# One ranking round in the router, router products spread over a wo2 unit, and waits moved in the experts' passes

## The reference, cut to what matters

```python
lg = t @ w_rg + b_rg                                  # 4 group scores per token
g_sel = argmax(lg);  w_grp = softmax(lg)[g_sel]
le = (t @ w_re + b_re).reshape(-1, 4, 4)              # 4 groups x 4 experts
le_g = le[g_sel]                                      # the chosen group's four
top_v, top_i = top_k(le_g, 2)
w_top = softmax(top_v) * w_grp                        # the two gates
for e in range(16):                                   # D = 1024, hidden = 512
    y = (silu(t @ w1[e]) * (t @ w3[e])) @ w2[e]
    acc += gate[e][:, None] * y
x = rmsnorm(x + g2 * acc, final_g)
```

## Time and profile before

| | |
|---|---|
| timed runs, median of 3 | 1209.31 us (1208.77 to 1213.37) |
| profiled execution | 1205.35 us |
| its span, first to last instruction | 1203.2 us |
| mean granted TensorE clock | 0.988 |
| TensorE busy | 1153.4 us (96%) |
| VectorE busy | 663.2 us (55%) |
| ScalarE busy | 499.2 us (41%) |
| GpSimd busy | 87.0 us (7%) |
| chain that ended last, by engine | PE 85%, DVE 9%, ACT 3%, issue 2% |

### The profile page before, as it was taken

The page is one execution under the profiler, slowest core; times in us unless marked ns, Lnnn a source line. Parts: engine busy times, 40 slices in busy tenths (PEclk is TensorE's granted clock), DMA queues, the critical chain, the costliest instruction groups (busy, mean ns, idle before and its releaser), DMA issues.

```text
span 1203.2 us, 21401 instructions
## 1 busy us (share of the span) xinstructions
PE 1153.4 (96%) x8936; PEld 996.9 (83%) x8936; DVE 663.2 (55%) x1143; ACT 499.2 (41%) x797; POOL 87.0 (7%) x92
## 2 busy tenths in 40 slices
PE   7999899999999989999999999999999899999996
PEld 6998789998979969999979889767899766665764
DVE  5777875588866476665555342775557531221223
ACT  5766523644374555544445222667344311111112
POOL 2451320000000100000100000000002000000000
PEclk9999999999999999999999999999999899999998
DMA  9544240443514746555564321302857899999980
GB/s 368 206 143 175 71 176 1 141 154 131 189 54 152 270 176 245 189 196 184 202 245 175 116 94 71 141 2 114 340 181 299 335 422 421 420 420 420 422 366 36
DMA packets 36204, 254.59 MB, mean 212 GB/s; under 512 B 4048, under 2 KB 4192, under 8 KB 5904
## 3 DMA queue, kind: packets, MB, share of 16 engines
q1 hardware_dynamic: 33552, 237.84, 51.4%
q0 software_dynamic: 2560, 15.42, 3.3%
HBM read 252.19 MB, written 1.05 MB: 210 GB/s over the span
## 4 chain that ended last, share of the span: by engine, by line
PE 85%; DVE 9%; ACT 3%; issue 2%; DMA 0%; DVEq 0%; ACTq 0%
PE bank L1374 13%; PE bank L712 12%; PE bank L706 12%; PE bank L707 12%; PE bank L668 5%; PE bank L1096 5%; PE bank L1182 4%; PE bank L1103 3%; PE bank L1386 2%; PE bank L759 2%; PE bank L1406 2%; PE bank L728 1%; PE bank L883 1%; DVE ring_low L2101 1%; PE bank L1284 1%
## 5 line engine op out<-in xcount | busy, mean ns | idle before, releaser
L2101 DVE TENSOR_TENSOR ring_low<-ring,w_high 128x2048 fp32r<-128x2048 f32 x104 | 238.0, 2290 | 160.8 <-ACT w_high L1629 160.7
L1629 ACT ACTIVATE w_high<-ring 128x2048 fp32r<-128x2048 f32 x104 | 199.1, 1915 | 281.5 <-PE bank L712 192.9
L706 PE MATMUL bank<-nT_high,w_high 128*128 128x256 f32 (+1 forms) x448 | 114.6, 295 | 0.0
L706 PEld LDWEIGHTS bank<-nT_high,w_high 128*128 128x128 f32 x448 | 84.2, 188 | 2.6 <-issue 2.4
L1374 PE MATMUL bank<-more,xs 128*64 128x256 f32 x768 | 84.6, 379 | 0.0
L1374 PEld LDWEIGHTS bank<-more,xs 128*64 128x64 f32 x768 | 58.7, 137 | 25.7 <-issue 2.2
L706 PE MATMUL bank<-hcl,w_high 128*128 128x256 f32 (+1 forms) x272 | 73.1, 306 | 0.0
L707 PE MATMUL bank<-hcl,w_high 128*128 128x256 f32 (+1 forms) x272 | 71.2, 299 | 0.0
L707 PE MATMUL bank<-nT_low,w_high 128*128 128x256 f32 (+1 forms) x272 | 64.7, 280 | 0.0
L706 PE MATMUL bank<-nMs,w_high 128*128 128x256 f32 x256 | 60.3, 280 | 1.4 <-DVE nMs L2493 1.4
L1096 PE MATMUL bank<-up,w_high 128*128 128x256 f32 x512 | 60.7, 276 | 0.0
(11 more groups left out here) (565 smaller groups left out, 2479.5 us busy)
## 6 DMA issues: line engine op xcount, KB each, us to landing
ring<-stream SPq DMA_DIRECT2D x163, 1024.0 KB, 4.9
more<-stream SPq DMA_DIRECT2D x60, 1024.0 KB, 18.7
more<-stream POOLq DMA_DIRECT2D x10, 1024.0 KB, 15.0
c<-constants_one SPq DMA_DIRECT2D x1, 1657.0 KB, 16.2
qc<-h_in SPq DMA_DIRECT2D x4, 272.0 KB, 3.8
c<-constants_two POOLq DMA_DIRECT2D x1, 1056.0 KB, 9.0
beside<-stream POOLq DMA_DIRECT2D x1, 1024.0 KB, 13.0
hT<-h_in POOLq DMA_DIRECT2D x1, 1024.0 KB, 6.0
```

The source lines that it names most:

```text
L706: nc.tensor.matmul(into[j], w, high_x(k), start=first, stop=False, skip_group_check=True)
L1629: A(w_high[:, d % 2, :], ring[:, s, :], ACT.Copy).then_inc(high_ready, 1)
L2101: TT(ring_low[:, s, :], ring[:, s, :], w_high[:, d % 2, :], sub).then_inc(low_ready, 1)
```

## The change

The diff does these things:

- Router: the two rankings become one over ten rows of four (two tokens' tiles of one group row and four expert rows), in a tile `beats` of its own that lies over `rB`, which is not in use then. The flag of the first group then selects both the experts' scores and their places. The arguments of the gates' exponentials become a function, `gate_arguments`, called after the first choices and the copy of the counts.
- wo2, unit 3: the products of blocks 0 to 5 are no longer made in one go halfway; block by block they are put among the products with the rounded weights (`among_wo2`). The sums of squares get a function of their own.
- Experts: the scatter waits for each half of the result by itself; in pass 0 the choices are turned before the hidden rows; the wait for the gates' column stands before the second half of the down products; in the extra pass only half of the scatter stands in front, the other half behind the up products; and the wait for the extra pass's gates moves from its start to where they are used.
- Pads: STAGGER grows from 16 to 48 words, a pad is added in front of `y_dsa_low`, and the pad under `more` grows by 16.

```diff
-STAGGER = 16
+STAGGER = 48
+        with ExitStack() as same:
+            beats = sb(same, "beats", 128, 10, 4, 8)
+                _stagger_dsa = sb(m, "stagger_dsa", 128, STAGGER)
...
                 for k in range(KT):
                     k_ready(k)
+                    among(k)
...
+            def router_squares(blocks):
+                dst = psum[banks.at["router"]]
+                pe.wait_ge(partial_ready, 3)
+                for k in blocks:
...
                 elif u == 3:
-                    router_blocks(range(6))
+                    router_squares([5])
+            def among_wo2(u, k):
+                blocks = {0: [0], 1: [1], 2: [2], 3: [3], 5: [4], 7: [5]}.get(k)
+                if u == 3 and blocks:
+                    router_blocks(blocks)
...
             router_blocks(range(6, KT))
+            router_squares(range(6, KT))
...
-            def scatter(count, signal=False, first=False):
-                pe.wait_ge(ys_ready, count * 2 + 2)
-                pe.wait_ge(spread_ready, count + 1)
-                for ft in range(KT):
+            def scatter(count, signal=False, first=False, fts=range(KT)):
+                if fts[0] == 0:
+                    pe.wait_ge(spread_ready, count + 1)
+                for ft in fts:
+                    if ft % 4 == 0:
+                        pe.wait_ge(ys_ready, count * 2 + 1 + ft // 4)
...
-                    scatter(count - 1)
+                    scatter(count - 1, fts=range(4))
...
+                if first:
+                    turn_choices()
+                    turn_hidden()
+                else:
+                    scatter(count - 1, first=(n == 1), fts=range(KT) if n < PAIRS else range(4, KT))
+                    turn_hidden()
+                    turn_choices()
...
-                pe.wait_ge(gate_slot_ready, count * 2 + 2)
                 for q in range(2):
+                    if q == 1:
+                        pe.wait_ge(gate_slot_ready, count * 2 + 2)
...
-                pe.wait_ge(gates_loaded, 2 * x + 2)
                 expert_pass(PAIRS, x, x + PAIRS, lambda qt: gate_of[:, qt, :])
...
+            five = rflat(0, 40).rearrange("p (s j) -> p s j", j=4)
+            step(TT(beats[:, :, :, 0:4], inner5, outer5, ALU.is_ge))
+            step(TT(beats[:, :, :, 4:8], inner5, outer5, ALU.is_gt))
+            step.settle()
+            step(TT(beats[:, :, :, 0:4], beats[:, :, :, 0:4], ahead.unsqueeze(1).to_broadcast([128, 10, 4, 4]), mul))
+            step(TT(beats[:, :, :, 4:8], beats[:, :, :, 4:8], behind.unsqueeze(1).to_broadcast([128, 10, 4, 4]), mul))
+            step.settle()
+            now(nc.vector.tensor_reduce(places.rearrange("p (s j) -> p s j", j=4), beats[:, :, :, :], AX, add))
+            now(TS(r2(72), place_of_group, 0.0, None, ALU.is_equal))
...
+            step(TT(among, logits[:, :, 4:20].rearrange("p q (g e) -> p q g e", e=4), outer(r2(72)), mul))
+            step(TT(among_places, place_in_group.rearrange("p q (g e) -> p q g e", e=4), outer(r2(72)), mul))
             step.settle()
+            step(nc.vector.tensor_reduce(r2(96), among.rearrange("p q g e -> p q e g"), AX, add))
+            step(nc.vector.tensor_reduce(r2(104), among_places.rearrange("p q g e -> p q e g"), AX, add))
+            def gate_arguments():
...
                     picks(place_in(0), pick_first)
                     CP(rt[:, 22, 0:16], bank[:, 32:48]).then_inc(free("rank"), 1)
+                    gate_arguments()
                     take_rows(0)
```

More of the change, by code:

```diff
@@ L1435, in expert_pass, with turn_hidden, turn_choices @@
                     gather_blocks(range(KT), 2 * CAP)
-                    scatter(count - 1)
+                    scatter(count - 1, fts=range(4))
                     for q in range(2):
                         half_rows(n, again, 2 * q, psum[q][:, 0:256], xs[:, :, 0:2 * CAP], KT, UNIT_COLS, rows_ready if q == 0 else lambda k: None)
[L1439 to L1448, removed]
+                def turn_hidden():
+                    pe.wait_ge(hid_rows_ready, count + 1)
+                    for k in range(4 if n < PAIRS else 2):
+                        last = nc.tensor.transpose(psum[2][:, k * 128:(k + 1) * 128], hid_rows[:, k * 128:(k + 1) * 128], ident)
+                    last.then_inc(hid_full, 1)
+                def turn_choices():
+                    pe.wait_ge(again_ready, count * 4 + 4)
+                    for qt in range(2):
+                        nc.tensor.transpose(psum[3][:, qt * 128:(qt + 1) * 128], pick_again[:, qt, :], ident)
+                    if n == PAIRS:
+                        pe.wait_ge(gates_loaded, 2 * again + 2)
+                    group(psum[3][:, SEQ:SEQ + 2], [(pick_again[:, qt, :], gates(qt)) for qt in range(2)]).then_inc(spread_full, 1)
+                if first:
[5 more added lines that the diff above has]
+                    turn_choices()
                 if n == 0:
@@ L2708, in _ @@
+            step.settle()
+            places = rflat(264, 40)
+            now(nc.vector.tensor_reduce(places.rearrange("p (s j) -> p s j", j=4), beats[:, :, :, :], AX, add))
+            place_of_group, place_in_group = places.rearrange("p (q n) -> p q n", n=20)[:, :, 0:4], places.rearrange("p (q n) -> p q n", n=20)[:, :, 4:20]
+            now(TS(r2(72), place_of_group, 0.0, None, ALU.is_equal))
             for qt in range(2):
-                STT(member[:, qt], over(r2(104)[:, qt, :], 4), 2.0, each(r2(72)[:, qt, :], 4), ALU.is_lt, mul).then_inc(routed_ready, 1)
+                STT(member[:, qt], place_in_group[:, qt, :].rearrange("p (g j) -> p g j", j=4), 2.0, each(r2(72)[:, qt, :], 4), ALU.is_lt, mul).then_inc(routed_ready, 1)
@@ L2716, in _ @@
+            among_places = rflat(560, 32).rearrange("p (q g e) -> p q g e", g=4, e=4)
+            step(TT(among, logits[:, :, 4:20].rearrange("p q (g e) -> p q g e", e=4), outer(r2(72)), mul))
+            step(TT(among_places, place_in_group.rearrange("p q (g e) -> p q g e", e=4), outer(r2(72)), mul))
             step.settle()
-            TT(r2(80), lg, one(64), sub).then_inc(rexp_arg_ready, 1)
-            now(TT(r2(144), r2(152), r2(96), mul))
-            now(nc.vector.tensor_reduce(rflat(160, 2), r2(144), AX, add))
@@ L2720, in _ @@
-            TT(rflat(180, 2), rflat(160, 2), rflat(120, 2), sub).then_inc(rexp_arg_ready, 1)
+            step(nc.vector.tensor_reduce(r2(96), among.rearrange("p q g e -> p q e g"), AX, add))
+            step(nc.vector.tensor_reduce(r2(104), among_places.rearrange("p q g e -> p q e g"), AX, add))
+            def gate_arguments():
+                step.settle()
+                step(nc.vector.tensor_reduce(rflat(64, 2), lg, AX, ALU.max))
+                step(TS(r2(112), r2(104), 0.0, None, ALU.is_equal))
+                step(TS(r2(152), r2(104), 1.0, None, ALU.is_equal))
+                step(nc.vector.tensor_reduce(rflat(120, 2), r2(96), AX, ALU.max))
+                step.settle()
+                TT(r2(80), lg, one(64), sub).then_inc(rexp_arg_ready, 1)
+                now(TT(r2(144), r2(152), r2(96), mul))
+                now(nc.vector.tensor_reduce(rflat(160, 2), r2(144), AX, add))
+                TT(rflat(180, 2), rflat(160, 2), rflat(120, 2), sub).then_inc(rexp_arg_ready, 1)
```

16 lines of the change are left out of this document (6 added, 10 removed).

## The result

The changed kernel takes 1189.88 us (median of 4 runs, 1189.58 to 1191.01), the kernel before in the same set 1210.34 (1208.77 to 1213.37): a ratio of 0.983, 95% interval 0.9808 to 0.9852. Two later sets gave 1189.80 and 1190.17 us.

A forecast was written before the change was run, and what follows sets the result against it. The prediction took TensorE, busy for 96% of the span, as the bound. Its terms, -0.85 + 0.55 - 0.59 - 2.3 - 6.6 + 0.1 = -9.7 us, took the timed 1209.31 to 1199.6, range 1194.5 to 1205.5.

The forecast's parts named there:

- The pads: Tiles behind the weights' copy move by 128 bytes or more: taken as nothing, ends about 10 us each way.
- The rival with the pads: Moved addresses put fast units on the slow pace, 4.3 ns a step, 19 us at 4464 steps: 1219; chance 0.07.
- one sign that the forecast named: Forecast wrong if units far ahead of the router changed their length, which would point to the pads; no size given.
- Ranking: Router: one ranking for two and fewer instructions behind it bring the first gather forward by 0.45 + 0.4 = 0.85 us.
- Router products: Last wo2 unit: spreading router products over six places costs six more returns at 0.09 us, +0.55 us.
- Pass 0: Experts' pass 0: choices' transposes go ahead of the hidden rows' into a wait of 0.9 us, -0.59 us.
- Odd passes: Passes 1, 3, 5, 7: first half of down products no longer waits for the gates' column, -0.58 us each, 2.3 in all.
- Extra pass and end: Five terms: gather's wait, clock, split scatter, a shorter wait, last scatter by halves; 6.9 us less 0.3, so -6.6.
- Loop entry: Extra pass: TensorE's entry into the loop may show once the gather's wait goes; bounds 0 and 1.8, taken as 0.3 us.
- The clock's 3.15: Extra pass: without the wait, gather and scatter run at the upper clock, 8.83 - 5.68 = 3.15 us.
- Weights: Weight stream: gains after pass 0 do not move it, 2.2 us of slack in pass 7; 0.1 us lost, +0.1.
- Better rival: Router's first gather also runs at the upper clock, about 3.7 us instead of 5.44: 1197.9 us; chance 0.18.

The follow-up runs named there:

- null: The kernel before, unchanged, run against itself: 1207.62 us against 1207.27, ratio 1.0006.
- after_no_pads: The changed kernel with the pads as before (STAGGER 16, no pad ahead of y_dsa_low): 1195.99 us.
- the first pad alone: The kernel before with only the pad ahead of nT, nMs and up at 48 words, not 16: 1204.13 us, ratio 0.9964.
- after_no_dsa_pad: The changed kernel without the pad ahead of y_dsa_low: 1190.58 us.
- after_gates_first: The changed kernel with the wait for the extra pass's gates at the start of the pass again: 1197.68 us.
- the gaps filled: The changed kernel with 12 more products that nobody reads on TensorE, in the router's three idle gaps: 1188.58 us.
- fed_no_rank: The changed kernel with the router's three idle gaps filled by unread products and the two rankings as before: 1190.81 us.

## Why the prediction was wrong

The step that failed is "The pads": "I take nothing". They are worth 4 to 6 us: 1203.44 against 1207.27 alone, 1189.8 against 1195.99 in the changed kernel. The reason given was that units reading the same tiles run at both paces, "so the address of these is not what tells them apart". The observation was right and the inference wrong. In the traces the slow pace was there behind a stall both in null and in after_no_pads, and only the latter kept it, for some 175 us; so one address can go with both paces, and still the addresses change how often the slow one stays: 0 of 12 runs with the first pad alone, 12 of 23 without it. The rival with the pads had the right kind of price (4.3 ns a step over thousands of steps) but it was thought of as a loss only. "SBUF — State Buffer" of the Trainium skill ("SBUF: two separate sides") was read as "nothing at all"; it says that TensorE waits for no other engine, which no run here contradicts, but the runs show that 128 bytes change its pace, of which it says nothing. The measurement decides.

The second miss is the base. The sum was made against an execution of 1205.35 us and carried over to a median 4 us higher as a difference. But the kernel before is two populations, and the change removes the slower one; a difference from a profile that lies in the faster one cannot show that. Of the 4 us ahead of the router, 1.2 are there at 22 us, where null differs from the profiled execution of before by 1.1 at the same code; as much again comes by 215 us, where that execution had a lower clock (0.83 from 140 to 150 us) that null did not have. Only the last 1.5 are paces. Two more traces of the changed kernel show these (1.5 and 1.6), and the first pad alone brings none of them. So one sign that the forecast named for its being wrong did come: units far ahead of the router changed their length.

In the means of the table the whole change is worth 18.0 us; the 20.5 of the result have 2.2 from its four runs of the kernel before, whose median lies that much above the 1208.1 of the later sets. Of the 18.0, 10.7 are at full clock and 7.1 lower clock, where the forecast had 6.55 and 3.15. The pads are 2.2 (alone, against null) to 4.6 (taken out) of the 4.1 missed at full clock, and about 1 of the 4 missed in lower clock. The rest of these seems to lie in the router's stretch: from 930 to 960 us the granted clock was 0.89 in the execution that the sum was made against but 0.77 in null's, and it was 0.83 in three traces of the changed kernel and 0.94 in those of after_no_dsa_pad and after_gates_first. What decides between these levels stays open.

Point by point:
- *Ranking*: 0.85 forecast, 0.86 in the traces with the clock held; right. In the changed kernel's own profile the lower clock takes it back (+0.88 in the gather). Longer in the runs, open.
- *Router products*: +0.55 forecast, +0.13 in the trace (926.50 to 933.30 is 6.80; 930.47 to 937.14 was 6.67). Mis-sized: six returns cost 0.02 us each, not 0.09.
- *Pass 0*: -0.59, measured -0.67 (the wait 0.89 is now 0.18 with the choices under it). *Odd passes*: -0.58, measured -0.63 each (999.04 to 994.20 is 0.63 more than the pass's start gained). Right.
- *Extra pass and end*: -6.6, measured -7.3 (-7.97 less pass 7's 0.63). Loop entry, bounded by 0 and 1.8 and taken at 0.3, is 0; the second half of the last scatter waits 0.44. The clock's 3.15 was right for the experts' part (3.1).
- *Weights*: no wait on a DMA in any of these traces; the 0.1 cannot be told.
- *Better rival* (the first gather at the upper clock): not in the three traces of the changed kernel (6.28 to 6.32 us), but in two of variants with the same router (3.81), and in all four traces with the gaps filled.

## What to carry to other kernels

Take several executions of a tuned kernel before summing against one, and split each into span times clock and the rest: two populations at full clock can mean a state that an edit removes. An unexplained spread of paces at equal shapes is worth a try with a pad of 128 bytes, here half of what five moved waits gave. A wait on TensorE can cost the lower clock behind it on top of itself, so a short gap that cannot be closed may be filled with products that nobody reads; read the clock afterwards, for the time may hardly change.

## What the hardware showed that was not expected

- The same products at the same addresses run at 113 or 118 ns a step, and one execution stayed at the slower pace for some 175 us (510 against 525 products in 60 us, clock 1.00). With the tiles moved by 128 bytes, 0 of 24 runs fell into the slower population (0 of 12 by the first pad alone, where 12 of 23 unmoved runs of the same set did); unmoved (with null) 42 of 93, moved by 256 bytes 8 of 12.
- After a wait of 1.83 us the granted clock was at 0.50 to 0.55 for about 10 us of uninterrupted products (after_gates_first). In fed_no_rank a wait of 1.58 us, with the gaps around it filled, left the clock at 1.00.
- The same router gaps gave a first gather of 3.81 us in some executions and 6.28 to 6.72 in others, by where the lower clock began and ended.
